# Moving layer 2's modulation sums from TensorE beside the experts to VectorE in layer 1's convolution stage

## What is computed

```python
cond_lat = jax.nn.silu(c)
cond_ctx = jax.nn.silu(c_ctx)
for l in range(DEPTH):
    mod_lat = (cond_lat @ w_mod[l] + b_mod[l])[:, None, :]
    mod_ctx = cond_ctx @ w_mod[l] + b_mod[l]
    sh1, sc1, gt1, sh2, sc2, gt2 = jnp.split(mod_lat, 6, axis=-1)
    csh1, csc1, cgt1, csh2, csc2, cgt2 = jnp.split(mod_ctx, 6, axis=-1)
    h = _rmsnorm(x, g_norm1[l]) * (1.0 + sc1) + sh1
    hc = _rmsnorm(ctx, g_norm1[l]) * (1.0 + csc1) + csh1
    p = h @ w_in[l]
    ...
    f = _peer(tok, peer_wq[l], peer_subkeys[l], peer_u[l], peer_v[l])
    x = x + gt2 * f[:B * S].reshape(B, S, D)
```

## Time and profile before

| what | us |
|---|---|
| median of three runs | 5167.25 |
| lowest and highest of them | 5164.17, 5177.09 |
| the profiled execution | 5149.73 |
| its span in the trace | 5147.9 |
| layer 1's convolution stage, first matmul to the next phase's first | 304.2 to 518.9 |
| modulation beside the experts | 2501 to 2661 |

### The profile page before, as it was taken

One profiled execution on the slowest core, in us unless ns is written; L12 is line 12 of the kernel. 1 busy time (PEld: TensorE's weight loads), 2 busy tenths in 40 slices (PEclk: granted clock), 3 DMA queues, 4 the chain that ended last, 5 costly groups with the idle time before them and its releaser, 6 DMA issues. The chain is left out here.

```text
span 5147.9 us, 66276 instructions
## 1 busy us (share of the span) xinstructions
PE 3732.3 (72%) x22132; PEld 1994.1 (39%) x22132; DVE 3526.2 (68%) x7189; ACT 2117.4 (41%) x5513; POOL 2390.9 (46%) x1707
## 2 busy tenths in 40 slices
PE   6899888677776666777688688768867776655555
PEld 2678358433332123553122254257833333211111
DVE  7532434778886877887558777764478887777776
ACT  5432114444454333445244444235444444444443
POOL 5112027566654335775333465204656665444443
PEclk8999898888887777998899898889888888777776
DMA  6011125899999989999999899823499999999998
GB/s 248 20 38 46 54 102 160 351 411 415 396 409 394 363 329 379 388 406 397 413 400 373 350 354 383 341 101 121 144 419 411 408 406 404 399 421 413 414 417 345
DMA packets 278130, 1639.43 MB, mean 318 GB/s; under 512 B 30356, under 2 KB 46420, under 8 KB 105500
## 3 DMA queue, kind: packets, MB, share of 16 engines
q0 software_dynamic: 184320, 1342.26, 64.3%
q1 hardware_dynamic: 93468, 292.93, 15.4%
HBM read 1611.32 MB, written 23.76 MB: 318 GB/s over the span
## 5 line engine op out<-in xcount | busy, mean ns | idle before, releaser
L576 POOL DMA_INDIRECT arena<-in_uv,arena x1280 | 1490.6, 1164 | 1666.9 <-PE psum L621 1273.8
L621 PE MATMUL psum<-arena 64*64 64x512 f32 x10240 | 1585.0, 746 | 864.3 <-ACT arena L600 842.7
L736 DVE SCALAR_TENSOR_TENSOR arena<-arena 128x1024 f32<-128x1024 f32 x1280 | 1743.5, 1362 | 615.8 <-DMA arena<-in_uv,arena 568.0
L1624 PE MATMUL psum<-view_at,view_at 128*128 128x256 f32 (+1 forms) x7968 | 1251.0, 313 | 125.7 <-POOL view_at L267 72.4
L1624 PEld LDWEIGHTS psum<-view_at,view_at 128*128 128x128 f32 x7968 | 1107.8, 200 | 498.9 <-issue 329.2
L267 POOL TENSOR_TENSOR view_at<-view_at,view_at 128x1024 fp32r<-128x1024 f32 x376 | 803.7, 2147 | 893.0 <-ACT view_at L360 543.1
L621 PEld LDWEIGHTS psum<-arena 64*64 64x64 f32 x10240 | 387.3, 156 | 1750.3 <-ACT arena L600 1156.2
L589 ACT ACTIVATE arena<-arena 128x1 f32<-128x1 f32 x1280 | 255.0, 199 | 1688.0 <-DVE arena L736 1623.0
L600 ACT ACTIVATE arena<-arena 128x64 f32<-128x64 f32 x1280 | 445.4, 348 | 88.8 <-PE psum L621 47.6
L360 ACT ACTIVATE view_at<-view_at 128x1024 fp32r<-128x1024 f32 x320 | 284.7, 891 | 333.4 <-DMA view_at<-in_w_in 141.4
L593 ACT ACTIVATE arena<-arena 128x1 f32<-128x1 f32 x1280 | 377.0, 295 | 46.4
(11 more groups left out here) (293 smaller groups left out, 3425.5 us busy)
## 6 DMA issues: line engine op xcount, KB each, us to landing
view_at<-in_w_in SPq DMA_DIRECT2D x180, 512.0 KB, 3.7
view_at<-in_w_mod SPq DMA_DIRECT2D x48, 1024.0 KB, 11.6
view_at<-in_w_br SPq DMA_DIRECT2D x120, 256.0 KB, 3.5
view_at<-in_w_out SPq DMA_DIRECT2D x40, 512.0 KB, 4.2
view_at<-in_wq SPq DMA_DIRECT2D x40, 512.0 KB, 9.7
arena<-in_uv,arena POOLq DMA_INDIRECT x1280
arena<-mod_rows SPq DMA_DIRECT2D x13, 512.0 KB, 9.3
arena<-in_keys SPq DMA_DIRECT2D x40, 128.0 KB, 8.4
```

The costliest lines, as they stand in the source:

```text
L576: nc.gpsimd.indirect_dma_start(out=self.slots[i % self.ring], out_offset=None, in_=self.table, in_offset=bass.IndirectOffsetOnAxis(ap=self ...
L621: last = nc.tensor.matmul(self.c.psum[tokens, at:at + 512], self.diag[rows, k % 4], self.slots[k % self.ring][rows, D + h * 512:D + (h + 1 ...
L736: nc.vector.scalar_tensor_tensor(out=self.junk, in0=self.slots[i % self.ring][:, 0:D], scalar=1.0, in1=self.h2_turned if i % 2 else self.h ...
L1624: last = nc.tensor.matmul(c.psum[:, at + lo:at + hi], a[:, k], b[:, k, lo:hi], start=(k == 0 and i == 0), stop=(k == kt - 1 and i == 2))
```

## The change

The sums over the 1024 rows of `w_mod` are split in two. In layer 1's convolution stage DVE multiplies a piece of 128 rows and 512 columns by the conditioning value of its row and adds it to a sum, eight pieces to a stream; twelve streams make the latents' modulation and four the context's shift and scale, 128 pieces in all. Each sum (128 partitions x 512) is stored to DRAM. In the stage beside the experts the 16 sums are loaded back, and PE adds up the partitions by 64 matmuls of one column. The pieces (256 KB each) have three places and the sums two; six pieces go with each of the first 21 jobs and two with the next.

```diff
@@ phase_mod_beside @@
-            for n in range(n_all):
-                if n >= SLOTS:
-                    sp.wait_ge(halves_done, n - SLOTS + 1)
-                sp.dma_start(raw[n % SLOTS], io["w_mod"][layer][n]).then_inc(w_landed[n % SLOTS], 16)
-                if n < len(moves):
-                    sp.dma_start(*moves[n]).then_inc(moved, 16)
+            for i in range(PARTS):
+                sp.dma_start(acc[:, i * each:(i + 1) * each], sums[:, i * each:(i + 1) * each]).then_inc(sums_in[i], 16)
+            for move in moves:
+                sp.dma_start(*move).then_inc(moved, 16)
...
-                pe.wait_ge(w_landed[n % SLOTS], 16 * (n // SLOTS + 1))
-                for k in range(HALF):
-                    last = nc.tensor.matmul(c.bank(q % 2, 512, 2), c.cond[:, half * HALF + k], raw[n % SLOTS][:, k * 512:(k + 1) * 512],
-                                            start=(half == 0 and k == 0), stop=(half == 1 and k == HALF - 1))
+                m = n - FIRST
+                if m >= 0:
+                    if m % each == 0:
+                        pe.wait_ge(sums_in[m // each], 16)
+                    q, s = streams[m]
+                    for j in range(4):
+                        at = TURNED + 2 * (4 * q + j) + s
+                        last = nc.tensor.matmul(c.psum[:, at:at + 1], acc[:, m, j * P:(j + 1) * P], c.ones[:, 0:1],
+                                                start=True, stop=True)
@@ phase_conv_branches @@
-            ring.load(sp, proj)
+            def load_piece(i):
+                m, k = divmod(i, KD)
+                half, kk = divmod(k, KD // 2)
+                if i >= RAW:
+                    sp.wait_ge(piece_added, i - RAW + 1)
+                sp.dma_start(raw[:, i % RAW], io["w_mod"][layer + 1][2 * streams_mod[m][0] + half][:, kk * 512:(kk + 1) * 512]
+                             ).then_inc(piece_landed[i % RAW], 16)
...
+            for n in range(len(jobs)):
+                for i in range(PER_JOB * n, min(PER_JOB * (n + 1), n_pieces)):
+                    load_piece(i)
+                    if i >= KD + 2 and (i - 2) % KD == 0:
+                        store_sum((i - 2) // KD - 1)
+                if n + ring.ahead < len(jobs):
+                    ring.load(sp, proj, blocks=(n + ring.ahead,))
...
+            def add_piece(i):
+                m, k = divmod(i, KD)
+                w, out, scale = raw[:, i % RAW], acc[:, m % 2], c.cond[:, k, streams_mod[m][1]:streams_mod[m][1] + 1]
+                dve.wait_ge(piece_landed[i % RAW], 16 * (i // RAW + 1))
...
+                else:
+                    dve.wait_ge(piece_added, i)
+                    nc.vector.scalar_tensor_tensor(out=out, in0=w, scalar=scale, in1=out, op0=ALU.mult,
+                                                   op1=ALU.add).then_inc(piece_added, 1)
...
+                for i in range(PER_JOB * n, min(PER_JOB * (n + 1), n_pieces)):
+                    add_piece(i)
```

More of the change, by code:

```diff
@@ L1013, in _, with phase_mod_beside @@
                     in1=c.cols[:, g:g + KD].unsqueeze(2).to_broadcast([P, KD, 2]), op0=ALU.add, op1=ALU.mult).then_inc(mod_ready, 1)
-def phase_mod_beside(c, layer, lay, share, moves):
+def phase_mod_beside(c, layer, lay, share, moves, sums):
     nc, io = c.nc, c.io
[L1020 to L1024, removed]
+    n_all, FIRST, PARTS = 24, 8, 4
+    streams = mod_streams()
+    n_both = SC1 + KD
+    acc, turned_row = c.at(136, len(streams), 512), c.at(189, P)
+    each = len(streams) // PARTS
     TURNED = 3 * 512
@@ L1056, in _ @@
         def _(act):
[L1057 to L1061, removed]
             for n in range(n_all):
-                if n >= 3 and n % 2:
-                    keep((n - 3) // 2)
                 if n in (12, 23):
@@ L1068, in _ @@
                 share.scalar(act, n)
[L1069 to L1072, removed]
+            act.wait_ge(mod_turned, 1)
+            nc.scalar.activation(turned_row[0:N_MOD], c.psum[0:N_MOD, 0:P], ACT.Copy).then_inc(rows_made, 1)
             share.scalar(act, n_all)
@@ L1086, in _ @@
         def _(pe):
[L1087 to L1093, removed]
[L1095 to L1104 removed]
+            for n in range(n_all):
+                m = n - FIRST
[7 more added lines that the diff above has]
+                                                start=True, stop=True)
+                        share.tensor(pe, n, j, 5)
+                    last.then_inc(summed, 1)
                 if n in (2, 13):
                     mlp.tensor(pe, n // 13)
[L1107 to L1108 removed]
                 share.tensor(pe, n)
[L1110 removed]
             pe.wait_ge(mod_ready, 2)
[L1112 to L1113 removed]
+            nc.tensor.transpose(c.psum[0:N_MOD, 0:P], c.mod[:, :, 0], c.ident[:]).then_inc(mod_turned, 1)
             share.tensor(pe, n_all)
@@ L1447, in _, with mod_streams @@
                                           [P, KV_HEADS, 2, HD])).then_inc(ready, 1)
+def mod_streams():
+    return [(q, 0) for q in range(N_MOD // 4)] + [(q, 1) for q in range((SC1 + KD) // 4)]
 def conv_jobs():
@@ L1628, in feature_job, with phase_conv_branches @@
     return last
[L1631 removed]
+def phase_conv_branches(c, layer, next_sums):
     nc, io = c.nc, c.io
@@ L1654, in phase_conv_branches @@
         mirrored = ph.sem("mirrored")
+        piece_landed = [ph.sem(f"mod_piece_landed{i}") for i in range(RAW)]
+        piece_added = ph.sem("mod_piece_added")
+        sum_stored = [ph.sem(f"mod_sum_stored{i}") for i in range(2)]
         def cols(base, tap, tile, tiles):
@@ L3375, in build @@
         lay = Mixing(c, apart=True)
-        moves = first_stages_beside(c, 1, lay, experts, latents)
+        moves = first_stages_beside(c, 1, lay, experts, latents, mod_sums)
         phase_qkv(c, 1, False, lay, moves)
```

54 lines of the change are left out of this document (34 added, 20 removed).

## The result

The changed kernel takes 5205.98 us (median of four runs, 5202.81 to 5208.15) against 5171.69 us for the kernel before in the same four rounds (5164.17 to 5177.09). The ratio is 1.0067, with a 95% interval of 1.0049 to 1.0084: slower by 34 us. The forecast was slower by 17 us, 5184 in a range of 5152 to 5210.

The account below looks back on a forecast made before the run. PE was taken to bound the convolution stage and DMA bytes the phase beside the experts. A cost of 57 us less a gain of 40 gave +17, from 5167.25 to 5184 us, range 5152 to 5210.

Parts of the forecast that it names:

- the ring: Convolution stage: a block's load waits for DVE's pieces, they for a block's rounding; 11.69 us a long turn, PE 8.35.
- Rival 1: Convolution stage: DVE's idle time takes the pieces, no ring closes; gain of 40 to 51 us stays, 5122 us; chance 0.07.
- Rival 3: Convolution stage: queued pieces and blocks make each turn 1 us longer; 19 us more, net +36, 5203 us; chance 0.12.
- my middle: Convolution stage: cost of 57 us, taken between 50.5 with quiet landing and 63.8 with 0.7 us more in 19 turns.
- The forecast's own case: Whole kernel: cost 50 to 64 us, gain 38 to 51, net 0 to +26; chance 0.57.
- The gain: Beside the experts: 20.98 MB less, 51.4 us at 408 GB/s, up to 13.1 lost to POOL's angle instructions; 40 us taken.
- Rival 4: Beside the experts: POOL stalls worse or later phases use freed bytes partly; gain 25 us, net +32, 5199; chance 0.10.
- The cost: Convolution stage: PE reaches job 21 later because turns exceed its 8.35 us a job; 57 us taken.
- the block's way: Convolution stage: w_in block from SP's issue to ACT's rounding, 3.72 us in quiet, 0.7 us more allowed under load.
- the quiet sum: Convolution stage: turns added up with quiet landing; PE starts job 21 at 229.0 us instead of 178.5, cost 50.5.
- POOL's split: Convolution stage, short convolution: stops DVE's instructions with two SBUF tensors for its whole 2.40 us, from a row at 4212 us.
- rival 2: Convolution stage: splitting on POOL costs DVE little; a triple takes 25.6 us, cost 38, net about 0, 5165; chance 0.14.

Follow-up runs that it names:

- e3: Changed kernel with SP loading the w_in block ahead of the job's fourth piece, not behind its sixth; 5178.27 us, ratio 1.002 to the kernel before.
- e5: Changed kernel with six places for pieces instead of three and nothing else; 5154.01 us, ratio 0.9994 to the kernel before.
- e8: Changed kernel with six places, block's load ahead of the third piece, low half copied by ACT instead of split by POOL; 5127.38 us, ratio 0.9943 to before.
- e4: Changed kernel with the low half of a block copied by ACT a turn later instead of split by POOL; 5185.12 us, ratio 1.0035 to before.
- e9: Changed kernel with six places, block's load ahead of the third piece, 128 pieces dealt evenly over 24 jobs; 5134.98 us, ratio 0.9952 to before.

## Why the prediction was right, and what it mis-sized

**The bound and the mechanism held.** The kernel became slower, through the ring that was forecast. PE's row of 15 jobs broke, the issues of L293 came every 10 to 14 us (15.6 the first time) right behind a piece, ACT's eviction stood behind a rounding that had waited for `w_in`, and moving one line in SP's list (e3) or adding places (e5) took 30 and 48.5 us off. Rival 1, that the pieces hide, was wrong for this order, but e8 shows that its condition was a possible one: with the circle open, nothing is lost. Rival 3, the DMA queue as the pace, was wrong as a bound (e8 moves the same bytes in less time) and right as a price: its cost of 76 us and its net of +36 are close to what came, as the turns were 0.7 us (short part) and 1.1 us (long part) longer than in my middle. The forecast's own case, a cost of 50 to 64 us and a net of 0 to +26, did not come. The difference of the medians is 34 us, twice the forecast's 17, and the time lies 4 us inside the upper end of its range. The sign is owed to the mechanism; that the time still fell into the range is owed to a wide range.

**The gain** was taken as 40 us and is 41.4. The working holds as well: the bytes alone would have given 51 us, and 10 of these are not covered (13.1 were estimated for POOL's angles). Its gathers beside the angles came 2.90 and 3.04 us apart, where 3.03 was taken. Rival 4 did not come.

**The cost** was taken as 57 us and is 76.1. The term that was mis-sized is the block's way, from issue to rounding. I had 3.72 us from a quiet row and 4.4 from the last part of the earlier trace rows; it was 5.33 in the median of 20. For 19 turns that is 1.61 x 19 = 30.6 us over the quiet sum, which gives 229.0 + 30.6 = 259.6 for the start of job 21. It started at 253.9. The other 5.7 us are mainly the other links, which came out smaller: in the mean 6.41 us a short turn (6.83 in the forecast) and 7.65 a long one (7.97). In the short turns the split was priced at 2.40 us and counted for 1.5 by e4. By the share of DMA the stretch that I scaled from and this one are nearly alike (51% in the earlier trace rows, 53 to 64% here), and the way is not: here each block is issued with 2.8 pieces in the mean still under way ahead of it.

**POOL's split** lies between the sum (all of it) and rival 2 (none). One case of each, in the timelines of DVE and of POOL:

```profile
337.52 5.28 DVE L1785 SCALAR_TENSOR_TENSOR arena<-arena,cond 128x512 f32<-128x512 f32 x4 [0.99 <-DMA arena<-in_w_mod]
...
360.89 2.48 DVE L1580 SCALAR_TENSOR_TENSOR arena<-arena,cols 128x511 f32<-128x511 f32 x2 [2.51 <-ACT arena L1747]
```

```profile
338.08 2.46 POOL L267 TENSOR_TENSOR view_at<-view_at,view_at 128x1024 fp32r<-128x1024 f32 x1 [13.79 <-ACT view_at L301]
...
360.04 2.40 POOL L267 TENSOR_TENSOR view_at<-view_at,view_at 128x1024 fp32r<-128x1024 f32 x1 [8.27 <-ACT view_at L301]
```

Four pieces take 5.28 us beside a split where four alone take 4 x 0.78 = 3.1, and the `xs` convolution's pair 2.48 instead of 1.15, because it started 0.85 us after the split did. The longest piece instruction lasted 2.81 us. So the single instruction does wait the split out, as the row at 4212 us said, and at most what is left of the split when DVE arrives is lost: 1.3 us for the `xs` convolution, 1.5 to 2.1 for pieces, and 1.5 us in the mean of a short turn. The GPSIMD Engine Reference of the Trainium skill says (section 1, Specifications) that instructions with two SBUF inputs contend with POOL. This case's trace agrees, with these 1.3 to 2.1 us.

**Not priced:** the granted clock. I wrote that I price no fall from 1.00. It fell to 0.92, 0.71 and 0.84 in the stretches in which PE waited, each a mean over time at 2.4 and at 1.2 GHz, and a job then took 10.2 us instead of 8.6. In the ring PE had the time; what the fall cost at the end is within 1 us (job 21 took 9.30, and from its start to the end of the stage it is 37.0 us against 36.2 before). In e8, where PE does not wait, the row is 0.99 again. So the fall came with the waits and went with them.

The forecast's time was 22 us too low: 19 from the stage's term, less 1.4 from the gain, and 4.4 from the median of before, which a fourth run moved from 5167.25 to 5171.69.

## What to carry to other kernels

Free busy time of an engine is not free room for work: write down, for each queue that the moved work passes through, what stands behind it and on whom it waits, and follow the chain until it ends or bites its own tail; if it does, its length against the stage's pace is the price. The two cheapest cures were in the list and not in the work: issue the critical load ahead of the one that waits, and give the added loads as many places as keep them from waiting for the same turn. Take a landing time from a load that had as many others under way ahead of it as the change will put there, not from one with a similar mean share.

## What the runs showed of the hardware

- A load of 512 KB went from issue to rounding in 3.72 us in quiet, in 4.00 with pieces of 64 KB ahead of it, and in 5.33 with pieces of 256 KB (stretches of 172 to 209 GB/s). The mean rate does not set it (e8: 4.45 us at 224 GB/s, e9: 5.44 at 212); it grew from 3.7 us with nothing under way ahead of the block to 6.0 with five or six loads of 256 KB.
- SCALAR_TENSOR_TENSOR on 128x512 in float32 takes 0.75 us, and up to 2.81 beside POOL's TENSOR_TENSOR of 2.40 (2.92 in e9). With PSUM as its source it is not stopped: none of the eleven 511-wide ones beside a split in the changed kernel took over 0.75 us. TENSOR_SCALAR of the same size, with one tensor less, takes 0.48 us alone, but it is stopped too: 2.5 to 2.6 us for three of them in e3. Both stand in one place of e9:

```profile
453.91 1.14 DVE L1584 SCALAR_TENSOR_TENSOR arena<-psum,cols,arena 128x511 f32<-128x511 f32 x2
454.97 1.35 DVE L1790 TENSOR_SCALAR arena<-arena,cond 128x512 f32<-128x512 f32 x1
```

```profile
453.63 2.40 POOL L267 TENSOR_TENSOR view_at<-view_at,view_at 128x1024 fp32r<-128x1024 f32 x1 [3.08 <-ACT view_at L301]
```

- Beside the experts PE's granted clock was 0.93 with the wide matmuls of `w_mod` and is 0.66 without them, while the phase became 41 us shorter. What a higher clock would have given there was not tried.
